# Output and query weights shared by two token tiles: a straight program in which a pair's expert rows last two steps

## The chip, the cores and the metric

The kernel runs on one core of a Trainium2 chip. The metric is the device time of one execution in microseconds (us), lower is better. The engines are TensorE (PE), VectorE (DVE), ScalarE (ACT), GpSimd (POOL) and SyncE (SP); SP, ACT and POOL issue transfers, which 16 DMA engines carry out.

## The reference

Two layers over 512 tokens of width 1024, everything in float32. Each layer is a token mixer (gated delta rule, short convolution, differential attention) with one input and one output projection, and then an expert retrieval:

```
for l in range(DEPTH):                       # 2
    proj = rms_norm(h, attn_norm[l]) @ w_in[l]              # 1024 -> 3592
    mixed = concat(gdn_mixer(...), short_conv_mixer(...), diff_attention(...))   # all causal
    h = h + mixed @ w_out[l]                                # 1024 -> 1024
    n = rms_norm(h, ffn_norm[l])
    q = n @ w_q                                             # 1024 -> 2048, 8 heads x 2 halves
    scores = q . sub_keys                                   # 2 x 128 keys for each head
    # top 16 of each half, top 16 of their 256 sums -> 128 experts per token, softmax gates
    hid = gelu(n . u_tab[idx])                              # 128 dot products per token
    h = h + sum(gate * hid * v_tab[idx])                    # 128 weighted rows per token
```

Each token has its own 128 experts, so for a tile of 128 tokens 128 gathers fetch rows of `peer_u` and 128 gathers rows of `peer_v`, each of 128 x 1024 floats (0.524 MB). Eight tiles (two layers of four) make 2048 such gathers, 1074 MB.

## The kernel before

**Tiles and steps.** Step t (0 to 7) computes the mixer and the expert choice of tile t; tiles 0 to 3 are layer 0, tiles 4 to 7 layer 1. The gathers of tile t are consumed beside step t+1 and, after step 7, in a tail of their own. Steps 0 and 1 are written out, steps 2 to 7 are a loop with two steps in its body, "lead" (2, 4, 6) and "follow" (3, 5, 7), and step 8 is the tail.

**Rows.** POOL gathers into a ring of 16 slots (`ring`), in a fixed order, each time a slot is free. A U row (from `peer_u`) is consumed by one dot product on DVE (`dot`, L1109). V rows (from `peer_v`) are consumed four at a time, as a unit, by eight matmuls on PE (`rows_v`, L810); their coefficients need all 64 dots of a half tile, a gelu, gates, and blocks that ACT writes (L507).

**What sets the order.** A string in `PLAN` says for each kind of step at which named place of the mixer U rows, V units and the small steps stand: L, H (row numbers of a half tile for the V gathers, ACT), G (gelu), C (coefficients), S (add the sums). `mix(name)` on each engine issues what the plan has there. POOL takes the rows in just that order. Engines run their own instructions strictly in order, and meet at the end of each step (`meet`).

**One step**, in the stretches that the text names:
- *projection*: norm, then `w_in` in 8 blocks of 449 columns. A lead step does it for two tiles, t and t+1, with one load of the weights; a follow step has none. Step 0 does its own tile, and tile 1 at its end.
- *conv*: convolution taps and gates, up to the transposes of the convolved values.
- *delta*: the delta rule's triangular inverse, six levels of small matmuls (L796) with DVE and ACT between.
- *attention*: state update, then four heads; logits over all 512 key positions, with a window of the bias strip copied by ACT (L606).
- *output*: `w_out`, 2 blocks; residual; second norm.
- *query*: `peer_wq`, 4 blocks, then transposes and key scores.
- *select*: top 16 searches and index arithmetic on DVE (`select`, L1117 to L1372), in two halves.

**Weights.** SP streams all weights through a ring of four slots (`wring`, L364), two transfers for each block: 16 for `w_in`, 4 for `w_out`, 8 for `peer_wq`. In before each tile's output and query blocks are loaded for that tile alone; ACT loads the keys once per step.

Of the kernel before, what the change touches and what calls it, by code (L numbers as in the profile page):

```python
# [38 lines left out]
STRIP = 896  # L39
# [7 lines left out]
EARLY = 4  # L47
# [3 lines left out]
W_ITEMS = 28  # L51

PG, PA, P_CW, P_SW, P_ON, P_QG, P_SUB, P_NA, P_DT, P_LAM, P_OFF = 0, 1024, 1032, 1080, 1086, 1214, 1278, 1342, 1346, 1350, 1351
P_W = 1352
# [4 lines left out]
PROJ = {"solo": (["nT0", "nT1"] + [f"pj{b}" for b in range(4)], [f"pj{b}" for b in range(4, 8)]),  # L59
        "lead": (["nT0", "nT1", "kT0", "kT1"] + [f"{n}{b}" for b in range(4) for n in ("pj", "pk")], [f"{n}{b}" for b in range(4, 8) for n in ("pj", "pk")]),  # L60
        "follow": ([], [])}
MIXERS = (["sT0", "sT1", "gcum", "grow"]
          + ["cN0", "cN1", "cN2", "qhT", "khT", "kbT", "kk", "qk", "qgT", "X0"]
          + [f"{n}{m}" for m in range(1, LEVELS - 1) for n in ("X", "D", "DT")] + ["dT", "X6", "DT6"]
          + ["wT", "vn", "oo", "sn", "lg00", "lg01", "yT", "lg10", "lg11"]
          + [n for h in range(2) for n in (f"aT{h}", f"lg{h+2}0", f"lg{h+2}1", f"pv{h}")] + ["aT2", "pv2", "aT3", "pv3", "zT"]
          + ["op0", "op1", "mT0", "mT1"] + [f"wq{i}" for i in range(4)] + [f"qT{i}" for i in range(4)] + [f"sc{i}" for i in range(4)])

SELECT = "sc:G r0:V r1:V r2:CV r3:V r5:V r9:V r11:V r13:V r15:V r17:V r20:V r21:V"
PLAN = {
    "first": "n0:LVVVVVVVVVVVVUUUUUU pj0:UUUU pj1:UUUU pj2:UUUU pj3:UUUU xT:UUU pj4:UUU pj5:UUU pj6:UUU pj7:UUU conv:UUU cN:UUU kbT:UUU X0:UUU "
            "L1:UUUU L2:UUUU L3:UUUU L4:UUUU L5:UUUG L6:SUU wT:C vn:UUV sn:UV y:V at1:UUUUUV at2:UUUUUV at3:UUUUUV pv3:UUUUUV op0:UUUUUUUUH op1:UUUUUV nm:UU "
            "wq0:UUUUU wq1:UUUUU wq2:UUUUU wq3:UUUUU " + SELECT,
    "lead": "n0:L n1:UUUUUUUU pj0:UUUUUUU pj1:UUUUUUUV pj2:UUUUUUU pj3:UUUUUUUV xT:U pj4:UUUU pj5:UUUUV pj6:UUUUV pj7:UUUUUUUUU conv:V "
            "cN:UV kbT:UV X0:V L1:UUUV L2:UV L3:UV L4:UGV L5:U L6:UUS wT:C vn:UUUUUV sn:V y:V at1:UUUUUV at2:UUUUUV at3:UUUUU pv3:UUUUU op0:UUUUUUUUH op1:UUUUUV nm:U "  # L80
            "wq0:UUUUUU wq1:UUUUUV wq2:UUUUU wq3:UUUUV " + SELECT,
    "follow": "n0:LUUUUUUV pj0:UUUU pj1:UUUU pj2:UUUU pj3:UUUU xT:UUV pj4:UU pj5:UUV pj6:UU pj7:UUV conv:UUV cN:UUV kbT:UUV "
              "X0:UUV L1:UUUV L2:UU L3:UUV L4:UU L5:UUV L6:UUU vn:UUUUUUU sn:UUUV y:GSC at1:UUUUVV at2:UUUUUVV at3:UUUUUVV pv3:UUUUU op0:UUUUUUUUUHV op1:UUUUUU nm:UU "
              "wq0:UUUUUUU wq1:UUUUUUU wq2:UUUUUUU wq3:UUUUUUUV " + SELECT,
    None: "end:L" + "UUUUUV" * 12 + "UUUUGUUUUSHUUUUC" + "UUUUV" * 14 + "GVVC" + "V" * NV}


def sequence(plan, first=False):

    out, row, n = [], 0, dict.fromkeys("ULHGCS", 0)  # L90
    n["V"] = EARLY
    for part in plan.split():
        where, kinds = part.split(":")
        for kind in kinds:
            if not (first and kind == "V" and n["V"] < NV):
                out.append((where, kind, n[kind], row))
# [6 lines left out]
def rows_of(seq):
    return [(kind, n) for _, kind, n, _ in seq for _ in range({"U": 1, "V": UNIT}.get(kind, 0))]


ORDER = {**{m: sequence(PLAN[m]) for m in PLAN}, "first": sequence(PLAN["first"], True), "solo": []}
LAST = rows_of(ORDER["first"])[-SLOTS:]
assert all(rows_of(ORDER[m])[-SLOTS:] == LAST for m in ("lead", "follow"))

# [15 lines left out]


def build(nc, x, rel_bias, attn_norm, w_in, gdn_conv, gdn_a_log, gdn_dt_bias, gdn_out_norm, sc_conv, diff_q_norm,
# [7 lines left out]
    with ctx:  # L136
# [3 lines left out]
        def sem(name):  # L140
# [9 lines left out]
        n2A = sb("n2A", D)  # L150
# [11 lines left out]
        carry = sb("carry", PAIRS)  # L162
# [4 lines left out]
        idxU, idxR = sb("idxU", K, i32), sb("idxR", K, i32)  # L167
        gateU, hid, coefR = (sb(n, K) for n in ("gateU", "hid", "coefR"))
# [1355 lines left out]
```

## Time and profile before

| | |
|---|---|
| median of 3 runs | 3429.05 us (3428.15 to 3433.24) |
| profiled execution, span | 3422.5 us |
| busy: PE / DVE / POOL / ACT | 2081.0 / 2265.7 / 2008.6 / 858.5 us |
| DMA | 1275.65 MB, mean 373 GB/s; the gathers 1075.38 MB of it |
| steps 0, 1 | 293.5, 357.3 us |
| steps 2, 3, 4 | 411.5, 376.0, 419.0 us |
| steps 5, 6, 7 | 376.7, 421.8, 371.8 us |
| tail | 394.9 us |

A step ends where DVE copies the normed tile for the dot products (L1424). The rows further down are windows of the trace between such points: for each the busy time of the engines with their instruction counts, the clock that was granted to TensorE (1.00 is 2.4 GHz, 0.50 is 1.2 GHz), the busy share of the DMA engines (full is 1.03 by this count) and the rate.

### The profile page before, as it was taken

What the parts mean: (1) busy time and instruction counts of PE and PEld (TensorE: products, weight loads), DVE (VectorE), ACT (ScalarE), POOL (GpSimd) and SP (SyncE); (2) the same over time, 40 slices, a digit from 0 to 9 for tenths busy, and PEclk for the clock granted to TensorE, in tenths of its full rate; (3) what the DMA queues carried; (4) which work ended last, traced back from release to release, by engine and by line L of the source; (5) the groups of instructions that cost most, each with busy time, mean ns of one, the idle gap of its engine ahead of it and who ended that gap; (6) DMA issues with size and microseconds to landing.
All of it is one profiled execution on the core that took longest, in us unless ns stands there. A gap on an engine that the chain in (4) does not pass through costs nothing.

```text
span 3422.5 us, 33690 instructions
## 1 busy us (share of the span) xinstructions
PE 2081.0 (61%) x9182; PEld 959.1 (28%) x9182; DVE 2265.7 (66%) x5019; ACT 858.5 (25%) x2516; POOL 2008.6 (59%) x2086
## 2 busy tenths in 40 slices
PE   7684466596673655497674556578776365633235
PEld 4541432244320322143331232133432132200001
DVE  3439965866759775775759876766677786675540
ACT  3311241322322230322313231223322232210111
POOL 1005454656647765665657766565665776577675
PEclk9797678698786878799787677889878687865666
DMA  9169789999999999999999999999999999999999
GB/s 300 71 208 391 238 318 401 385 400 406 378 402 409 405 353 402 405 366 404 378 402 408 407 350 405 405 363 401 369 394 405 409 391 373 406 409 409 411 409 362
DMA packets 395336, 1275.65 MB, mean 373 GB/s; under 512 B 37523, under 2 KB 78553, under 8 KB 393857
## 3 DMA queue, kind: packets, MB, share of 16 engines
q0 software_dynamic: 295744, 1075.38, 80.1%
q1 hardware_dynamic: 97808, 187.52, 15.1%
q10 hardware_dynamic: 1584, 10.47, 0.8%
q8 instruction: 80, 1.31, 0.2%
q14 instruction: 120, 0.98, 0.1%
HBM read 1266.24 MB, written 6.98 MB: 372 GB/s over the span
## 4 chain that ended last, share of the span: by engine, by line
DMA 29%; PE 24%; DVE 20%; issue 12%; POOL 11%; ACT 4%; PEldq 0%; POOLq 0%; DVEq 0%; ACTq 0%; SPq 0%; PEld 0%
DMA ring<-in_peer_v,idxR 13%; PE work L823 12%; POOL ring L438 11%; DVE ring L1109 8%; DMA ring<-in_peer_u,idxU 7%; DMA wring<-in_peer_wq 5%; PE accs L810 4%; DMA wring<-in_w_in 4%; PE work L796 3%; PE work L787 2%; DVE proj L1121 1%; PE work L934 1%; DVE proj L1117 1%; ACT arena L479 1%; DVE arena L1287 1%
## 5 line engine op out<-in xcount | busy, mean ns | idle before, releaser
L1109 DVE CUSTOM_DVE_ANT_0 ring<-ring,n2U 128x1024 f32<-128x1024 f32 x1024 | 1214.3, 1219 | 425.0 <-DMA ring<-in_peer_u,idxU 396.2
L438 POOL DMA_INDIRECT ring<-in_peer_u,idxU x1024 | 989.3, 966 | 758.1 <-issue 286.5
L438 POOL DMA_INDIRECT ring<-in_peer_v,idxR x1024 | 1002.9, 979 | 611.5 <-issue 267.9
L810 PE MATMUL accs<-ring,wv 128*32 128x512 f32 x4096 | 719.7, 838 | 737.3 <-DMA ring<-in_peer_v,idxR 698.0
L823 PE MATMUL work<-wring,nT 128*128 128x512 f32 (+1 forms) x1408 | 669.8, 633 | 122.8 <-DMA wring<-in_peer_wq 86.4
L810 PEld LDWEIGHTS accs<-ring,wv 128*32 128x32 f32 x4096 | 148.7, 135 | 1226.0 <-issue 1083.5
L823 PEld LDWEIGHTS work<-wring,nT 128*128 128x128 f32 x1408 | 289.3, 211 | 492.8 <-issue 377.8
L507 ACT ACTIVATE wv<-stack,coefR 128x32 f32<-128x32 f32 x1024 | 237.8, 309 | 379.1 <-PE accs L810 374.1
L479 ACT ACTIVATE arena<-work 128x512 f32<-128x512 f32 (+1 forms) x208 | 116.7, 588 | 462.8 <-PE work L787 236.2
L479 ACT ACTIVATE proj<-work 128x512 f32<-128x512 f32 (+1 forms) x120 | 68.1, 581 | 534.9 <-PE work L823 517.8
L1117 DVE MAX8 proj<-proj 128x8 f32<-128x128 f32 x256 | 52.7, 278 | 162.0 <-ACT proj L479 161.2
L787 PE MATMUL work<-ident,arena 128*128 128x128 f32 x296 | 61.1, 356 | 146.5 <-DVE arena L1296 107.0
L823 PE MATMUL work<-wring,arena 128*128 128x449 f32 x384 | 148.8, 540 | 0.0
L796 PE MATMUL work<-arena 128*128 128x128 f32 x768 | 109.6, 297 | 33.0 <-issue 22.8
L787 PE MATMUL work<-ident,proj 128*128 128x128 f32 x360 | 58.8, 314 | 113.2 <-DVE proj L1145 51.5
L796 PEld LDWEIGHTS work<-arena 128*128 128x128 f32 x768 | 99.0, 206 | 53.8 <-issue 42.0
L823 PEld LDWEIGHTS work<-wring,arena 128*128 128x128 f32 x384 | 72.8, 190 | 72.2 <-issue 72.2
L787 PEld LDWEIGHTS work<-ident,arena 128*128 128x128 f32 x296 | 45.8, 186 | 167.9 <-DVE arena L1296 121.7
L787 PEld LDWEIGHTS work<-ident,proj 128*128 128x128 f32 x360 | 47.0, 161 | 141.5 <-DVE proj L1145 55.7
L1109 DVE DVE_READ_ACCUMULATOR2_ANT hid<- 128x1 f32 x1024 | 84.4, 82 | 0.0
L1287 DVE CUSTOM_DVE_ANT_0 arena<-work,arena 128x512 f32<-128x512 f32 x64 | 44.3, 692 | 57.8 <-PE work L934 53.9
L681 ACT ACTIVATE idxR<-idxU 32x16 int32<-32x16 int32 x256 | 58.2, 227 | 83.4 <-DVEq L1393 49.3
(264 smaller groups left out, 2083.7 us busy)
## 6 DMA issues: line engine op xcount, KB each, us to landing
wring<-in_w_in SPq DMA_DIRECT2D x80, 898.0 KB, 15.7
wring<-in_peer_wq SPq DMA_DIRECT2D x64, 1024.0 KB, 20.0
wring<-in_w_out SPq DMA_DIRECT2D x32, 1024.0 KB, 19.9
ring<-in_peer_u,idxU POOLq DMA_INDIRECT x1024, 11.5
ring<-in_peer_v,idxR POOLq DMA_INDIRECT x1024, 12.0
arena<-keys_scr ACTq DMA_DIRECT2D x8, 1024.0 KB, 8.9
strip_scr<-ring SPq DMA_DIRECT2D x4, 512.0 KB, 8.2
keys_scr<-ring SPq DMA_DIRECT2D x2, 1024.0 KB, 5.0
```

The costliest lines, as they stand in the source:

```text
L438: nc.gpsimd.indirect_dma_start(ring[:, s * D:(s + 1) * D], None, table, bass.IndirectOffsetOnAxis(ap=idx, axis=0)).then_inc(row_in[s], 16)
L479: nc.scalar.activation(dst, s, ACT.Copy, **kw).then_inc(free[BANK[mode[0]][name][0]], 1)
L507: nc.scalar.activation(wv[:, d * QUARTER:(d + 1) * QUARTER], stack[:], ACT.Copy, scale=coefR[:, kk:kk + 1]).then_inc(blocks_ready, 1)
L681: ins = nc.scalar.activation(halves(dst, c)[quarter(o), q, :], src[quarter(q), columns(c, o)], ACT.Copy)
L787: ins = nc.tensor.transpose(w[:, i * P:(i + 1) * P], s, ident[:])
L796: ins = nc.tensor.matmul(w[:, i * P:(i + 1) * P], l, r, start=True, stop=True)
L810: ins = nc.tensor.matmul(acc[c][quarter(r), :], wv[:, d * QUARTER:(d + 1) * QUARTER], ring[:, s * D + 512 * c:s * D + 512 * c + 512], star ...
L823: ins = nc.tensor.matmul(w[:, 0:n], left[:, kc * P:(kc + 1) * P], wslot(i, n)[:, k, :], start=(kc == 0), stop=(kc == 7))
L934: filled(name, nc.tensor.matmul(w[:], qTa[o:o + 32, b * P:(b + 1) * P], keyT[o:o + 32, b * SEQ:(b + 1) * SEQ], start=True, stop=True))
L1109: V.tensor_tensor_reduce(out=rw, in0=rw, in1=n2U[:], scale=1.0, scalar=0.0, op0=ALU.mult, op1=ALU.add, accum_out=hid[:, kk:kk + 1]).then_i ...
L1117: ins = V.max(out=vals[:, 16 * i + o:16 * i + o + 8], in_=src[:, w * i:w * i + w])
L1287: link(V.tensor_tensor_reduce(out=lgs[:, o:o + 512], in0=w[:], in1=win[:, 512 * h:512 * h + 512], scale=1.0, scalar=-3e38, op0=ALU.add, op ...
```

## The change

1. The loop is gone: all eight steps and the tail are written out, with tables by tile (`order_of_banks`, `WEIGHTS`) in place of registers.
2. Output weights, query weights, key load, scores and selection of tiles 2+3, 4+5 and 6+7 are done together at the end of steps 3, 5 and 7 (`TAILS`, `stage_t`). Steps 2, 4 and 6 end after attention. Tiles 0 and 1 keep a pass of their own. In step 3, 5 or 7 one weight block serves two products, one for each tile.
3. Since the experts of both tiles are known only at the end of the pair, the gathers of a pair last over the next two steps. Rows consumed by step, tail last: before 0, 208, 256, 256, 256, 256, 256, 256, 304; now 0, 208, 121, 183, 192, 320, 192, 320, 512.
4. Attention takes only the keys up to the tile's own end: 128, 256, 384 or 512 wide for the four tiles of a layer. The window copies of ACT are gone, as DVE reads the strip directly.
5. Second buffers for what two tiles hold at once (`n2B`, `yscB`, `idxU1`, `gateU1`).

```diff
+FRONT = {0: (0,), 2: (2, 3), 4: (4, 5), 6: (6, 7)}
+BACK = {0: (1,)}
+TAILS = {0: (0,), 1: (1,), 2: (), 3: (2, 3), 4: (), 5: (4, 5), 6: (), 7: (6, 7)}
...
+LEAD = ("n0:RR n1:U8 pj0:U7 pj1:U7 pj2:U7 pj3:U7 xT:U pj4:U5 pj5:U5 pj6:U5 pj7:U5 conv:U3 cN:U2 kbT:U2G X0:U2 L1:U3C L2:U3V L3:U3V L4:U3V L5:U3V L6:U3V "
+        "vn:U6V sn:U3V y:UV at1:U6V2 at2:U6V2 at3:U6V2 pv3:U6V2 turn:U10G ")
+FOLLOW = ("n0:NCRVVU4 pj0:U4V pj1:U4V pj2:U4V pj3:U4V xT:U2V pj4:U4V pj5:U4V pj6:U4V pj7:U4V conv:U3V cN:U3V kbT:U3V X0:U3V L1:U3V L2:U3 L3:U3S L4:U3R L5:U2G L6:U2 "
+          "vn:U5C sn:U2V y:UV at1:U5V2 at2:U5V2 at3:U5V2 pv3:U4V op0:U8 op1:U8 nm:U wq0:U6 wq1:U6 wq2:U6 wq3:G sc:CNV "
+          "r0:V r1:V r2:V r3:V r5:V r7:V r9:V r11:V r13:V r15:V r17:V r20:V r21:V s0:V s1:V s3:V s5:V s7:V s9:V s11:V s13:V s15:V turn:S ")
...
+    2: "n0:R n1:U6 pj0:U3V pj1:U3V pj2:U3V pj3:U3V xT:U pj4:U3V pj5:U3V pj6:U3V pj7:U3V conv:U2V cN:UV kbT:U2V X0:UV L1:U3 L2:U3 L3:U2 L4:U2 L5:U2 L6:US "
+       "vn:U4R sn:U2 y:U at1:U4 at2:U4G at3:U4C pv3:U4",
+    3: "n0:U3 pj0:U pj1:UV pj2:U pj3:U xT: pj4:UV pj5:U pj6:U pj7:U conv:UV cN:U kbT:UV X0:U L1:U L2:UV L3:U L4:UV L5:U L6:U vn:U2V sn:U y:U at1:U at2:U2V at3:U2 pv3:U "
+       "op0:U6 op1:U6 nm:U wq0:U4 wq1:U3 wq2:U3 wq3:G sc:CN r0:V r1:V r2:V r3:V r5:V r9:V r11:V r13:V r15:V r17:V r20:V r21:V "
+       "s0:V s1:V s3:V s5:V s7:V s9:V s11:V s13:V s15:V s17:V s20:V turn:S",
+    4: LEAD, 5: FOLLOW, 6: LEAD, 7: FOLLOW,
+    8: "end:RR" + "U64" + "GU4C" + "U4V" * 15 + "NGVRU4C" + "U4V" * 15 + "GVSRU4C" + "U4V" * 15 + "GVC" + "V16S",
...
-            with sp.Fori(2, PAIRS - 1, 2) as j:
-                weights(j, "lead")
-                weights(j + 1, "follow")
...
+            def product(kind, b, who, left, n):
...
+                i0 = FIRST_ITEM[kind, b, who[0]]
+                for k in who:
+                    w = fill(f"{kind}{b}.{k}")
...
+                        if k == who[-1]:
+                            ins.then_inc(w_used, 1)
...
+        def keys_wide(k):
+            return P * (k % TILES + 1)
```

In these strings `R` is a half tile's row numbers (before: L and H), `N` the copy of the normed tile for the dots, a digit repeats the letter ahead of it, `r0` to `r21` are the places of the first tile's selection and `s0` to `s21` those of the second.

**TensorE at the end of a pair's second step.** `wring` are query weights, `proj` and `projB` the queries that are transposed, `arena` their products with the keys, `accs` the V units. Before (steps 3, 5, 7; all four query blocks, then on):

```order
L820 REGISTER_ALU
L823 MATMUL work<-wring,nT 128x512 x16
L820 REGISTER_ALU
L823 MATMUL work<-wring,nT 128x512 x16
L804 ISA
L806 ISA
L810 MATMUL accs<-ring,wv 32x512 x8
L787 MATMUL work<-ident,proj 128x128 x16
L796 MATMUL work<-arena 128x128 x16
L804 ISA
L806 ISA
L810 MATMUL accs<-ring,wv 32x512 x8
```

Now, in step 3 (the last three of the four query blocks):

```order
L836 MATMUL work<-wring,nT 128x512 x8
L836 MATMUL work<-wring,arena 128x512 x8
L836 MATMUL work<-wring,nT 128x512 x8
L836 MATMUL work<-wring,arena 128x512 x8
L836 MATMUL work<-wring,nT 128x512 x8
L836 MATMUL work<-wring,arena 128x512 x8
L800 MATMUL work<-ident,proj 128x128 x16
L809 MATMUL work<-arena 128x128 x16
L800 MATMUL work<-ident,projB 128x128 x16
L809 MATMUL work<-arena 128x128 x16
L823 MATMUL accs<-ring,wv 32x512 x192
```

Each query block is now two products, the transposes and scores come twice, no V unit stands among them, and 24 units (192 matmuls) follow in one piece beside the two selections.

**TensorE at the end of the program.** Before:

```order
L804 ISA
L810 MATMUL accs<-ring,wv 32x512 x8
L1060 REGISTER_ALU
L273 REGISTER_ALU
L273 COMPARE_AND_BRANCH
L810 MATMUL accs<-ring,wv 32x512 x352
L136 UNCONDITIONAL_BRANCH
```

Now:

```order
L836 MATMUL work<-wring,arena 128x512 x8
L800 MATMUL work<-ident,proj 128x128 x16
L809 MATMUL work<-arena 128x128 x16
L800 MATMUL work<-ident,projB 128x128 x16
L809 MATMUL work<-arena 128x128 x16
L823 MATMUL accs<-ring,wv 32x512 x696
L195 UNCONDITIONAL_BRANCH
```

Of the units behind the last loop step there were 44 (352 matmuls), all in the tail; of the 87 (696) now, 23 stand beside the selections of step 7 and 64 in the tail.

## Rows read from the trace of the kernel before

**Rows 1.** A window for each step, of all engines; steps 4 and 5 left out.

```profile
core 0: us, PE busy (x) PEld busy (x) DVE busy (x) ACT busy (x) POOL busy (x), PEclk, DMA share, GB/s
0.00:293.50 293.50, 226.71 (x818) 133.22 (x818) 139.59 (x410) 78.85 (x155) 31.49 (x54) 0.90 0.65 216
293.50:650.80 357.30, 185.67 (x820) 96.22 (x820) 276.60 (x617) 89.68 (x254) 198.96 (x205) 0.71 0.91 343
650.80:1062.30 411.50, 302.99 (x1276) 142.32 (x1276) 282.06 (x627) 114.60 (x332) 247.81 (x255) 0.84 1.01 394
1062.30:1438.30 376.00, 202.50 (x1000) 90.96 (x1004) 280.92 (x618) 96.75 (x292) 250.96 (x255) 0.77 1.00 394
...
2234.00:2655.80 421.80, 303.06 (x1272) 142.97 (x1268) 282.93 (x626) 114.80 (x332) 249.48 (x257) 0.83 0.99 386
2655.80:3027.60 371.80, 203.84 (x1020) 90.62 (x1015) 280.67 (x618) 96.39 (x292) 255.72 (x261) 0.78 1.00 396
3027.60:3422.50 394.90, 147.03 (x704) 28.67 (x704) 159.22 (x261) 55.99 (x235) 273.47 (x292) 0.63 1.00 399
```

**Rows 2.** A window in the tail: the rate of gathers alone.

```profile
3045.00:3345.00 300.00, 99.14 (x456) 18.99 (x452) 146.32 (x239) 39.07 (x163) 216.90 (x232) 0.62 1.03 410
```

**Rows 3.** DMA issues by line: count, size of one, us to landing.

```profile
wring<-in_w_in SPq DMA_DIRECT2D x80, 898.0 KB, 15.7
wring<-in_peer_wq SPq DMA_DIRECT2D x64, 1024.0 KB, 20.0
wring<-in_w_out SPq DMA_DIRECT2D x32, 1024.0 KB, 19.9
...
arena<-keys_scr ACTq DMA_DIRECT2D x8, 1024.0 KB, 8.9
```

**Rows 4.** Windows of step 0, without rows: delta, attention, scores.

```profile
80.00:129.00 49.00, 32.45 (x202) 29.11 (x200) 27.84 (x42) 12.19 (x25) 0.00 (x0) 0.79 0.35 125
129.00:172.80 43.80, 26.29 (x140) 19.18 (x140) 19.30 (x52) 20.24 (x43) 0.00 (x0) 0.74 0.12 48
...
226.50:232.00 5.50, 3.92 (x34) 3.67 (x33) 0.00 (x0) 3.26 (x6) 0.00 (x0) 1.00 0.70 243
```

**Rows 5.** Windows of step 1: conv stretch and before, delta, attention.

```profile
293.50:354.60 61.10, 8.63 (x38) 6.17 (x39) 55.08 (x89) 15.75 (x33) 35.80 (x34) 0.58 0.96 362
354.60:435.10 80.50, 38.79 (x202) 35.01 (x200) 73.41 (x127) 16.73 (x42) 36.19 (x38) 0.67 0.72 245
435.10:502.20 67.10, 43.55 (x220) 19.75 (x220) 43.56 (x94) 25.24 (x72) 38.17 (x41) 0.71 0.82 306
```

**Rows 6.** Windows of step 6: projection, delta, attention, select; then step 3's delta.

```profile
2257.00:2369.00 112.00, 109.70 (x332) 52.08 (x333) 78.19 (x125) 20.88 (x43) 67.38 (x70) 0.97 1.02 394
...
2380.00:2444.00 64.00, 42.08 (x312) 27.22 (x309) 46.82 (x73) 21.09 (x63) 42.87 (x44) 0.92 1.03 408
2444.00:2509.00 65.00, 42.77 (x188) 20.97 (x188) 43.76 (x96) 23.60 (x65) 38.60 (x40) 0.61 0.91 343
...
2596.00:2655.80 59.80, 28.82 (x180) 6.50 (x176) 57.82 (x227) 18.54 (x70) 39.71 (x41) 0.79 1.03 407
...
1133.80:1197.30 63.50, 42.59 (x298) 27.99 (x296) 52.83 (x85) 16.48 (x45) 48.86 (x49) 0.89 1.02 403
```

**Rows 7.** Timeline of TensorE: projection of two tiles starts; output; query; V unit.

```profile
665.94 9.29 PE L823 MATMUL work<-wring,nT 128*128 128x449 f32 x16 [1.72 <-ACT arena L488]
...
174.05 15.47 PE L823 MATMUL work<-wring,nT 128*128 128x512 f32 x32 [0.52 <-issue]
...
197.02 29.66 PE L823 MATMUL work<-wring,nT 128*128 128x512 f32 x64 [0.73 <-issue]
...
2265.89 6.20 PE L823 MATMUL work<-wring,arena 128*128 128x449 f32 x16
...
2284.11 1.92 PE L810 MATMUL accs<-ring,wv 128*32 128x512 f32 x16
```

**Rows 8.** Groups by line and shape: the dot product.

```profile
L1109 DVE CUSTOM_DVE_ANT_0 ring<-ring,n2U 128x1024 f32<-128x1024 f32 x1024 | 1214.3, 1219 | 425.0 <-DMA ring<-in_peer_u,idxU 396.2 <-ACTq L703 5.5 <-PEq L1059 4.4
```

More of the change, by code:

```diff
@@ L50 @@
 WSLOTS = 4
[L51 to L67, printed above, removed]
@@ L88, in sequence @@
[L88 to L96, printed above, removed]
+PG, PA, P_CW, P_SW, P_ON, P_QG, P_SUB, P_NA, P_DT, P_LAM = 0, 1024, 1032, 1080, 1086, 1214, 1278, 1342, 1346, 1350
+P_W = 1351
+MODE = ("solo", "follow") + ("lead", "follow") * 3
@@ L97, in sequence, with schedule @@
+def schedule():
+    out, row = {}, 0
+    per_tile = {"U": K, "V": 2 * NV, "R": 2, "G": 2, "C": 2, "S": 1, "N": 1}
+    n = dict.fromkeys(per_tile, 0)
+    for t in range(PAIRS + 1):
+        out[t] = []
+        for part in PLAN[t].split():
+            where, kinds = part.split(":")
+            for kind in each(kinds):
+                out[t].append((where, kind, n[kind] // per_tile[kind], n[kind] % per_tile[kind], row))
+                n[kind] += 1
                 row += {"U": 1, "V": UNIT}.get(kind, 0)
-            n[kind] += 1
@@ L99, in sequence @@
-    assert n["U"] == K and n["V"] in (2 * NV + EARLY, 3 * NV) and [n[k] for k in "LHGCS"] == [1, 1, 2, 2, 1] and row % SLOTS == 0
-    return out
[L103 to L109, printed above, removed]
+    assert all(n[k] == PAIRS * per_tile[k] for k in n), n
@@ L209, in build @@
+        full = [sem(f"bank_full{b}") for b in range(BANKS)]
+        free = [sem(f"bank_free{b}") for b in range(BANKS)]
         row_in = [sem(f"row{r}") for r in range(SLOTS)]
@@ L438, in gather, with step @@
                 nc.gpsimd.indirect_dma_start(ring[:, s * D:(s + 1) * D], None, table, bass.IndirectOffsetOnAxis(ap=idx, axis=0)).then_inc(row_in[s], 16)
-            def step(t, a, gathered, first=False):
-                if not gathered:
-                    return
-                before, seen = rows_of(order(a, first)), {}
-                for _, kind, n, row in order(a, first):
+            def step(t):
+                for _, kind, k, n, row in ORDER[t]:
                     if kind == "U":
@@ L885, in stage_a @@
+                flip(f"qgT.{k}", blocks(qn, 4))
+                pe.wait_ge(S["mx_ready"], nth("mx_ready", k))
+                heads(f"X0.{k}", [(mxa[:, h * P:(h + 1) * P], ident[:]) for h in range(GH)])
                 mix("X0")
@@ L1043, in _, with step @@
             pe.sem_inc(met, 1)
-            def step(t, a, gathered, first=False):
-                mode[0] = a
-                turn(a, first)
+            def step(t):
                 def mix(name):
-                    if not gathered:
+                    if t == 0:
                         prepare(name)
-                    for where, kind, n, row in order(a, first):
-                        if gathered and where == name and kind == "V":
-                            rows_v(t, first, n, row)
-                if not a:
+                    for where, kind, k, n, row in ORDER[t]:
+                        if where == name and kind == "V":
+                            rows_v(k, n, row)
+                if t == PAIRS:
                     mix("end")
```

1054 lines of the change are left out of this document (539 added, 515 removed), and 2 rows, old and new, of the table PLAN.

## The prediction

> **What bounds the kernel now.** I read the windows by step first. From step 2 to the end the DMA engines are busy 0.99 to 1.01 of the time at 386 to 399 GB/s, and in the tail, where nothing but gathers runs, 1.03 at 410 GB/s [rows 1, 2]. DVE is busy for about 280 of some 375 to 420 us in these steps, PE for 200 to 300 [rows 1]. So the transfers set the time of steps 2 to 8, and only steps 0 and 1 (216 and 343 GB/s) are set by their chains of work. A gathered row costs 0.5243 MB / 0.410 = 1.28 us of full rate [rows 2].
>
> Then I looked for the length of a step where it has little to gather, since the change makes such steps. Step 0 has no rows at all: delta 49.0 us, attention 43.8 us, with DVE busy 27.8 and 19.3 us of these [rows 4]. Here PE, ACT and DVE wait for each other in turn. Each row consumed inside adds to this chain: in step 1 delta takes 80.5 us with 30 dots, (80.5 - 49.0) / 30 = 1.05 each; in step 6 64.0 with 11 dots and 7 V units, 0.83 each; in step 3 63.5 with 20 and 6, 0.56 each [rows 5, 6]. Attention: step 1 67.1 with 23 and 7, 0.78 each; step 6 65.0 with 25 and 5, 0.71 each [rows 5, 6]. One dot is 1.22 us [rows 8], so little of it hides.
>
> **What the change removes.** Three passes of 4 + 8 weight transfers of 1024 KB (1.049 MB) and three of eight key loads of that size [rows 3]: 39 x 1.049 = 40.9 MB, 102 us at 0.40 MB/us, the rate of stretches with weights in them [rows 1]. The bill from step 2 on at full rate, after: 1840 rows x 1.28 = 2355, 48 loads of `w_in` (0.920 MB) x 2.3 = 110, 36 x 2.62 = 94, three key loads 8, in all 2567 us; before it was 2669, and took 3422.5 - 650.8 = 2771.7 [rows 1], so about 100 us, the end included, went unused.
>
> The Trainium skill (Perfetto Trace Analysis, section Identifying the Most-Contended Engine) says to relieve the engine with the highest use first; by that rule the 102 us would be the gain. The rows agree on which resource it is; whether it stays so in each step is counted below. The same page of the Trainium skill, section Optimization Strategy, advises to interleave stretches with different limits, and this change separates them.
>
> **What it moves.** The plan's counts: steps 2 and 3 consume 121 + 183 = 304 rows for 512 before, steps 4+5 and 6+7 still 512, the tail 512 for 304. 208 rows go from beside the mixers of steps 2 and 3 to the tail, where nothing hides them. What do steps 2 and 3 take without them?
>
> *Step 2.* Norms until the first projection product: 665.9 - 650.8 = 15 us [rows 1, 7]. Projection 112 [rows 6]: PE is busy for 110 of it, its blocks 2 x 6.2 us [rows 6, 7]; 7 V units for 4 add 3 x 1.9 [rows 7] = 6. Conv stretch 11 us in step 6 (between its windows of 2257 to 2369 and 2380 on, rows 6), take 12. Delta with 17 dots and 3 units: 49 + 20 x 0.65 = 62 (0.56 to 1.05 each: 60 to 70). Attention with 23 dots, 384 keys wide: 44 + 23 x 0.8 = 62, less 3 for the width, plus 4 for the row numbers and coefficients that ACT writes there = 63. End 4. Sum **274 us**. Its transfers would need 121 x 1.28 + 16 x 2.3 = 192, so DMA idles for some 80 us.
>
> *Step 3.* Up to the end of the conv stretch step 1 takes 61.1 with 40 dots [rows 5]; now 12 dots and 3 units: 28 dots fewer at 0.8 to 1.22 give 27 to 39, take 36 with the units. Delta, 9 + 3: 49 + 8 = 57. Attention, 11 + 2, full width: 44 + 10 = 54. Output: 15.5 us for one tile [rows 7], 31 for two; the second norm ends 5 us after the products for one tile, two share ACT, take 10: 41. Query: 29.7 for one tile [rows 7], 59 for two, and 4 for transposes. Scores of the first tile 5.5 [rows 4]; those of the second lie beside the selection. Selection: 59.8 us with DVE busy 57.8 of it [rows 6], twice: 120. End 3. Sum **380 us** against transfers of 183 x 1.28 + 12 x 2.62 + 3 = 268. The selections hold 96 rows, 123 us, and stay full; the output and query stretches, 110 us, hold 23 rows and 12 loads, 61 us.
>
> Steps 2+3 together: 654, before 411.5 + 376.0 = 787.5 [rows 1], **-133**. Of their transfer time of 460, nearly 200 us of DMA are left idle, twice what the removed loads save.
>
> *Steps 4+5, 6+7.* Lead step: 19 (as step 2, and 4 more for row numbers) + 104 (112 without its 4 units) + conv 15 + delta with 29 consumptions, dense on DVE, 49 + 29 x 0.93 = 76 + attention with 45, 44 + 34 = 78, less 10 (128 keys) or 4 (384) + 10 dots at the end 15: 297 and 303. In step 6 of before the loop's jump back shows as a start of 23 us for 15 (2234 to 2257, rows 1 and 6); that is gone here. Follow step: up to attention 193 rows, 247 us of transfers against a chain of some 225, take 243; then output 41, query 63, scores with copies and a V unit 11, selection 120, end 3: 481. Pairs: 778 and 784, before 795.7 (two steps alike left out of the rows) and 421.8 + 371.8 = 793.6 [rows 1]. **-27** together, not the 68 of removed loads, since in the 110 us of output and query there are 35 rows and 12 loads (76 us) and a ring that is at most 20 us ahead.
>
> *Tail.* 394.9 + 208 x 1.28 = **661, +266** [rows 1, 2]. PE (147 of 395 us busy) and DVE (159) stay far from a limit, with the same eight-row pattern.
>
> *Steps 0 and 1.* Attention is 128 and 256 wide for 512, and ACT's copies go. In the 43.8 us of step 0 [rows 4] I take 9 off (4 to 14); in step 1 the ring is full again from there on, 4 (0 to 9). **-13.**
>
> The second copies and buffers, the per-tile tables and missing register work cost nothing where transfers or a chain bind; I take 0 (up to 5 us either way).
>
> Sum: 3422.5 - 133 - 27 + 266 - 13 = **3515.5** for the span. The median of the runs lies 6.55 above the span, so **3522 us**, 2.7% slower.
>
> **The rivals.**
> - *Bytes are time (faster).* If every step stayed full, the 102 us come off: 3429 - 102 - 13 = 3314. It speaks for it that DMA is at its limit in every step now [rows 1]; against it that step 2 would have to end in 192 us while its projection alone needs 127. This is what the rule cited above from the Trainium skill (Perfetto Trace Analysis) would give. Chance 2%.
> - *Short chains (faster).* The rows inside hide as in step 3's delta, and pairs 4+5 and 6+7 come near their transfer time. Step 2 is then 15 + 104 + 10 + 49 + 41 + 17 = 236 at the least, step 3 345, the pairs 745 each: 3422.5 - 206 - 99 + 266 - 20 + 6.5 = 3370. It turns to a gain once steps 2 to 7 together are 93 us shorter than in my sum. For it: two tiles' chains meet fewer rows than any row of the trace shows beside step 0. Against: 0.56 is the lowest of five prices. Chance 7% for under -0.2%, and 3% for a stop within 0.2%.
> - *Longer still.* PE's clock was 0.61 in the attention of step 6 and 0.74 in step 0's [rows 4, 6]; if starved stretches keep it at 1.2 GHz in the doubled products too, 87 us of output and query in each pair cost up to twice as much: half of that is 130 us, 3650. Against: the solo products of step 0 ran at full pace after just such an attention [rows 7]. Chance 8% for over 3585.
>
> **How the numbers follow.** Forecast 80%: 3455 to 3585, from delta and attention at 0.56 to 1.05 per consumption (-25 to +35 over six steps), the transfer-bound part of the follow steps (up to 20 us of ring each, -40 to +10), steps 0 and 1 (-10 to +9). What a measurement can tell from no change is about 0.2%. Faster 0.09, same 0.03, slower 0.88; the predicted time is the forecast's, and the range 3455 to 3585 leaves out some 2 in 10.
>
> **What would show it.** In the changed profile: 40.9 MB less; step 2 near 274 us with the rate near 280 GB/s, step 3 near 380 with 290; output and query of steps 3, 5, 7 with PE over 0.9 busy and DMA under full; selections of 120 us; a tail of 661 us at 410 GB/s, with 64 units. I am wrong if step 2 and 3 sum to under 600, or if the pairs take under 740, since the chains then hide more than step 1 showed.

## The result and the profile after

The changed kernel takes 3552.7 us (3549.5 to 3554.8), beside 3428.6 us of the kernel before: a ratio of 1.036, 95% interval 1.0346 to 1.0375. It is slower by 3.6%; 3522 us were predicted, with a range of 3455 to 3585. The profiled execution spans 3547.5 us.

These are the windows by step of the changed kernel, in the columns of [rows 1], and one more in its tail, which answers to [rows 2]. The line from 2884.00 on is the tail. Here steps 3, 5 and 7 end with DVE's addition of the sums (L1420), steps 4 and 6 with the dot before the copy of the second tile (L1453), step 2 with attention.

```profile
core 0: us, PE busy (x) PEld busy (x) DVE busy (x) ACT busy (x) POOL busy (x), PEclk, DMA share, GB/s
0.00:277.90 277.90, 214.92 (x777) 127.21 (x778) 133.87 (x405) 71.52 (x151) 31.20 (x52) 0.90 0.67 220
277.90:635.50 357.60, 187.64 (x803) 96.10 (x801) 273.03 (x614) 84.86 (x250) 197.48 (x203) 0.70 0.91 341
635.50:886.00 250.50, 183.71 (x790) 102.37 (x790) 151.68 (x275) 75.27 (x201) 125.82 (x127) 0.83 0.91 338
886.00:1247.90 361.90, 247.59 (x1158) 120.93 (x1158) 253.25 (x705) 92.92 (x258) 178.57 (x176) 0.81 0.80 289
1247.90:1566.80 318.90, 200.56 (x832) 106.03 (x832) 210.45 (x383) 78.97 (x227) 182.34 (x192) 0.79 0.93 358
1566.80:2064.90 498.10, 293.19 (x1388) 127.04 (x1388) 340.41 (x856) 121.28 (x389) 315.91 (x323) 0.77 0.95 370
2064.90:2384.50 319.60, 203.46 (x856) 106.36 (x856) 213.56 (x382) 81.75 (x227) 181.17 (x190) 0.80 0.92 354
2384.50:2884.00 499.50, 297.30 (x1412) 127.86 (x1412) 343.41 (x857) 123.74 (x389) 314.85 (x323) 0.76 0.93 361
2884.00:3547.50 663.50, 212.29 (x1024) 41.84 (x1024) 314.92 (x520) 91.59 (x389) 470.28 (x502) 0.59 1.01 402
...
2900.00:3500.00 600.00, 188.81 (x888) 36.91 (x892) 298.26 (x492) 78.24 (x336) 437.49 (x467) 0.57 1.03 410
```

No step from 2 to 7 keeps the DMA engines full any more: 0.80 to 0.95, where [rows 1] had 0.99 to 1.01. The tail runs at the rate of [rows 2] and is about as long as its 512 rows (512 x 1.28 = 655).

| | before | predicted | after |
|---|---|---|---|
| steps 0+1 | 650.8 | 638 | 635.5 |
| steps 2+3 | 787.5 | 654 | 612.4 |
| steps 4+5 | 795.7 | 778 | 817.0 |
| steps 6+7 | 793.6 | 784 | 819.1 |
| tail | 394.9 | 661 | 663.5 |
| span | 3422.5 | 3515.5 | 3547.5 |

The count of 183 rows in step 3 is that of the kernel; the diff of the change above shows its plan with one dot less at `at1` (the kernel has `at1:U2`) and without `r7:V`.

From the page, the transfers and the weights' way (three groups of DMA issues, answering to [rows 3]), and the two dearest waits:

```profile
DMA packets 375573, 1231.47 MB, mean 347 GB/s; under 512 B 36866, under 2 KB 77896, under 8 KB 374512
...
L1133 DVE CUSTOM_DVE_ANT_0 ring<-ring,n2U 128x1024 f32<-128x1024 f32 x1024 | 1210.8, 1219 | 451.1 <-DMA ring<-in_peer_u,idxU 419.7
...
L453 POOL DMA_INDIRECT ring<-in_peer_v,idxR x1024 | 995.3, 972 | 701.0 <-issue 281.3
...
wring<-in_w_in SPq DMA_DIRECT2D x80, 898.0 KB, 8.3
wring<-in_peer_wq SPq DMA_DIRECT2D x40, 1024.0 KB, 12.1
wring<-in_w_out SPq DMA_DIRECT2D x20, 1024.0 KB, 13.4
```

44.2 MB less are moved, 40.9 of them the shared weights and keys, at 347 for 373 GB/s.

Now the stretches, which answer to [rows 4 to 6]. Step 2: projection, delta, attention. Step 3: output, query, and both selections.

```profile
650.50:765.00 114.50, 114.49 (x380) 52.90 (x380) 46.00 (x71) 23.91 (x58) 57.20 (x58) 0.98 1.00 375
...
771.00:831.30 60.30, 37.52 (x251) 28.53 (x249) 54.15 (x89) 13.26 (x29) 37.17 (x37) 0.83 0.92 353
831.30:886.00 54.70, 21.76 (x96) 14.98 (x96) 42.03 (x96) 22.98 (x66) 21.61 (x23) 0.57 0.67 220
...
1023.30:1065.00 41.70, 35.12 (x82) 16.59 (x82) 24.55 (x43) 5.04 (x11) 13.32 (x14) 0.83 0.87 303
1065.00:1120.00 55.00, 54.31 (x127) 24.21 (x128) 10.66 (x20) 6.05 (x10) 9.11 (x10) 1.00 0.61 212
...
1131.00:1247.90 116.90, 63.80 (x389) 14.16 (x387) 110.34 (x422) 27.20 (x111) 86.86 (x89) 0.80 0.98 389
```

Projection and query are PE's alone (busy 114.49 of 114.50, 54.31 of 55.00), the selections DVE's (110 of 117), and DMA idles beside attention and query. That is the chain-bound pair that was forecast. Steps 4 and 5 are different: delta and attention of step 4, then of step 5 all up to conv's end, delta, attention, output and query.

```profile
1377.20:1460.50 83.30, 43.91 (x282) 32.68 (x280) 64.13 (x109) 24.61 (x72) 40.11 (x42) 0.75 0.73 264
1460.50:1555.80 95.30, 46.39 (x249) 16.70 (x249) 52.78 (x118) 17.82 (x67) 71.80 (x78) 0.70 1.03 409
1566.80:1690.60 123.80, 45.64 (x222) 12.62 (x223) 69.27 (x112) 31.87 (x107) 89.85 (x91) 0.64 1.01 396
1690.60:1766.30 75.70, 45.48 (x266) 34.78 (x265) 59.73 (x96) 18.08 (x50) 48.32 (x48) 0.76 0.90 346
1766.30:1844.10 77.80, 39.65 (x229) 15.16 (x229) 48.08 (x107) 25.74 (x92) 52.98 (x57) 0.73 0.94 358
1844.10:1885.50 41.40, 34.13 (x87) 16.29 (x84) 27.89 (x49) 5.29 (x11) 23.84 (x25) 0.89 1.03 406
1885.50:1940.30 54.80, 54.80 (x128) 24.20 (x129) 19.30 (x34) 5.72 (x9) 16.11 (x18) 1.00 0.92 351
```

Within one step the limit changes from stretch to stretch. In step 4's delta POOL starts only 42 gathers in 83 us and DMA is at 0.73: the ring's slots are taken, and POOL waits 44.1 us for dots to free them. In its attention no engine is busy over 0.76 of the time, POOL included, but DMA is full, and DVE waits 29.5 us for rows. The two waits (total us, times, longest):

```profile
POOL ring L453 <- DVE hid L1133: 44.1, 9, 16.3
...
DVE ring L1133 <- DMA ring<-in_peer_u,idxU: 29.5, 4, 8.7
```

### The profile page after: what moved, and what is told of

It reads as the page before. It is cut to its first block, busy times and chain, and to the rows that moved or that the text cites. A ratio compares the mean times of both kernels' runs of the same rounds, so it can differ in the third digit from the quotient of the medians.

```text
span 3547.5 us, 30818 instructions
## 1 busy us (share of the span) xinstructions
PE 2040.7 (58%) x9038; PEld 955.7 (27%) x9038; DVE 2234.6 (63%) x4995; ACT 821.9 (23%) x2481; POOL 1997.6 (56%) x2084
## 4 chain that ended last, share of the span: by engine, by line
PE 31%; DVE 25%; POOL 15%; DMA 13%; issue 12%; ACT 4%; POOLq 0%; DVEq 0%; ACTq 0%
PE work L836 19%; POOL ring L453 15%; DVE ring L1133 8%; DMA ring<-in_peer_v,idxR 7%; PE accs L823 4%; PE work L809 4%; DMA ring<-in_peer_u,idxU 3%; DMA wring<-in_w_in 3%; PE work L800 2%; DVE projB L1145 1%; DVE projB L1141 1%; ACT arena L488 1%; DVE proj L1145 1%; DVE arena L1257 1%; ACT coefR L690 1%
## 5 line engine op out<-in xcount | busy, mean ns | idle before, releaser
L823 PE MATMUL accs<-ring,wv 128*32 128x512 f32 x4096 | 748.4, 869 | 940.0 <-DMA ring<-in_peer_v,idxR 873.0
L836 PE MATMUL work<-wring,nT 128*128 128x449 f32 (+1 forms) x1024 | 448.0, 593 | 33.9 <-DMA wring<-in_w_in 18.5
L836 PE MATMUL work<-wring,arena 128*128 128x512 f32 (+1 forms) x736 | 313.7, 577 | 11.7 <-DMA wring<-in_peer_wq 10.4
L836 PEld LDWEIGHTS work<-wring,nT 128*128 128x128 f32 x1024 | 203.1, 202 | 266.6 <-issue 240.2
L488 ACT ACTIVATE arena<-work 128x512 f32<-128x512 f32 (+3 forms) x224 | 120.2, 563 | 473.4 <-PE work L800 258.2
L836 PEld LDWEIGHTS work<-wring,arena 128*128 128x128 f32 x736 | 142.3, 194 | 174.4 <-issue 164.4
L488 ACT ACTIVATE proj<-work 128x512 f32<-128x512 f32 (+1 forms) x88 | 49.0, 576 | 279.3 <-PE work L836 275.4
L488 ACT ACTIVATE projB<-work 128x449 f32<-128x449 f32 (+1 forms) x64 | 36.6, 572 | 316.3 <-PE work L836 312.4
L809 PE MATMUL work<-arena,proj 128*128 128x128 f32 x384 | 68.1, 332 | 62.8 <-ACT arena L488 62.8
L1133 DVE DVE_READ_ACCUMULATOR2_ANT hid<- 128x1 f32 x1024 | 84.3, 82 | 0.0
L809 PEld LDWEIGHTS work<-arena,proj 128*128 128x128 f32 x384 | 58.3, 233 | 81.9 <-ACT arena L488 71.1
```

Source lines behind the costliest of these rows:

```text
L488: nc.scalar.activation(dst, s, ACT.Copy, **kw).then_inc(free[BANK[name][0]], 1)
L809: ins = nc.tensor.matmul(w[:, i * P:(i + 1) * P], l, r, start=True, stop=True)
L823: ins = nc.tensor.matmul(acc[c][quarter(r), :], wv[:, d * QUARTER:(d + 1) * QUARTER], ring[:, s * D + 512 * c:s * D + 512 * c + 512], star ...
L836: ins = nc.tensor.matmul(w[:, 0:n], left(k, kc), wslot(i, n)[:, kc % 4, :], start=(kc == 0), stop=(kc == 7))
L1133: V.tensor_tensor_reduce(out=rw, in0=rw, in1=n2U[:], scale=1.0, scalar=0.0, op0=ALU.mult, op1=ALU.add, accum_out=hid[:, kk:kk + 1]).then_i ...
```

## The experiments

Where nothing else is said, the kernel before took 3425.9 to 3429.2 us beside them.

**The single-tile kernel in a straight program.** `TAILS` gives each tile its own output, query and selection again, and the plan is that of the kernel before (L and H written R).

```diff
-TAILS = {0: (0,), 1: (1,), 2: (), 3: (2, 3), 4: (), 5: (4, 5), 6: (), 7: (6, 7)}
+TAILS = {t: (t,) for t in range(8)}
...
+    2: LEAD1, 3: FOLLOW1, 4: LEAD1, 5: FOLLOW1, 6: LEAD1, 7: FOLLOW1,
...
```

> The straight program and the narrow attention alone: each tile has its own output, query and selection pass again, and the order of rows is that of the kernel before (256 rows in each of steps 2 to 7, 304 in the tail). Theory A (the pairs cost all of the loss): before less 13 to 16 us for the narrow attention of steps 0 and 1 and less 2 x 7 us for the loop's jumps back, 3400 us (3385 to 3415). Rival C (the straight program or the new buffers cost something themselves): above 3430 us, up to 3550.

Measured: 3388.5 us, ratio 0.989 (0.9874 to 0.9907): 1.1% faster than the kernel before and 4.6% faster than the changed one, so all that makes the change slow is in the pairing and in the order of rows that goes with it. Its windows for steps 4 to 7 and the tail:

```profile
1420.50:1828.00 407.50, 293.96 (x1232) 139.14 (x1236) 277.05 (x623) 108.83 (x328) 244.95 (x254) 0.84 1.02 397
1828.00:2207.50 379.50, 208.48 (x1008) 94.38 (x1000) 276.69 (x615) 91.58 (x288) 255.92 (x264) 0.75 1.01 397
2207.50:2613.60 406.10, 297.37 (x1244) 139.96 (x1248) 280.62 (x623) 111.38 (x328) 242.99 (x250) 0.83 1.02 395
2613.60:2989.50 375.90, 212.41 (x1032) 94.92 (x1023) 280.54 (x616) 94.18 (x288) 259.04 (x264) 0.75 1.00 394
2989.50:3383.70 394.20, 142.99 (x704) 28.34 (x704) 159.34 (x260) 56.13 (x235) 273.50 (x292) 0.61 1.00 400
```

DMA is full in each, with all weights loaded per tile. Against this kernel the changed one stands at +164 us by the spans: steps 2+3 612.4 for 783.9, a tail of 663.5 for 394.2, together **+98**; pairs 4+5 and 6+7 817.0 and 819.1 for 787.0 and 782.0, together **+67**; steps 0 and 1 -1.

**One pair only.** The same, but tiles 6 and 7 are paired, with the plan of steps 2 and 3 and the long tail.

```diff
-TAILS = {t: (t,) for t in range(8)}
+TAILS = {**{t: (t,) for t in range(6)}, 6: (), 7: (6, 7)}
...
```

> As e3_single, but tiles 6+7 share one pass, with the plan that the changed kernel has for its first pair (steps 2 and 3) in steps 6 and 7, and its tail of 512 rows. Theory A (one shortage of rows, paid once, at the first pair wherever it stands): steps 6+7 near 612 us in place of some 775, the tail 663 for 395: about +100 us on e3_single, near 3500 us. Rival D (each pair costs the same): a third of the loss of the changed kernel against e3_single, +50 us, near 3450 us.

Measured: 3488.0 us, ratio 1.017 (1.0155 to 1.0189), 99.6 over the single kernel. Steps 6 and 7 take 250.8 and 360.6 us, 171 less than there, the tail 665.3, 271 more. Rival D (+50) is out: the 98 us come once, with the first pair wherever it stands, whose two steps have 304 rows to consume and leave 208 more to the tail.

**Width or loop?** The single kernel with attention over all 512 positions; the bias is then read at a wrong offset and future keys aren't masked.

```diff
         def keys_wide(k):
-            return P * (k % TILES + 1)
+            return SEQ
```

> The kernel of e5_wide once more (e3_single, 3388.5 us, with attention over all 512 key positions in every tile; bias read at the wrong offset in six tiles and future keys not masked, same work), since its first run fell where before took 3726 us. Theory A (a step set by transfers doesn't feel a shorter chain, only steps 0 and 1 do): step 0 gets 7 to 12 us longer, step 1 by 0 to 6, the others by under 2 each: 3403 us, between 3395 and 3412; the rest of the 39.7 us between e3_single and before is then the loop (its start in steps 4 and 6, and register work). Rival (the narrow attention made the whole gain): 3420 to 3430.

Measured: 3411.1 us, ratio 0.9957 (0.9941 to 0.9973), 22.6 over the single kernel, at the upper edge of what theory A gave; the rival is out. Step 0 is 12.0 longer, step 1 6.4, the pairs of steps 2+3, 4+5 and 6+7 by 6.5, -0.9 and -0.7: in the last two pairs a lead step's longer attention is given back in the follow step. About 23 of the 40 us are thus the narrow attention, 18 of these in steps 0 and 1. The other 15 are what else tells this kernel from the one before: the straight program and the missing window copies of ACT, which no run parts.

**The shared loads alone.** The changed kernel, but in steps 3, 5 and 7 each output and query block is loaded for each tile: 36 loads of 1.049 MB more, all else in place.

```diff
...
-                    product("op", i, tails, mixed, 512)
+                    for k in tails:
+                        product("op", i, (k,), mixed, 512)
...
-                    product("wq", i, tails, normed, 512)
+                    for k in tails:
+                        product("wq", i, (k,), normed, 512)
```

> The changed kernel, but in steps 3, 5 and 7 each output and query block is loaded twice, once for each tile of the pair (36 weight transfers of 1.049 MB more, 94 us of DMA time at 2.62 us each), with the same order of products and rows. Theory A (the saved transfers fall where the DMA engines are idle anyway): by the busy shares of the output, query and score stretches of the changed kernel, step 3 has 35 us idle there and steps 5 and 7 about 13 us each, so 0 + 18 + 18 = +37 us, 3590 us. Rival B (bytes are time): +94 us, 3647 us.

Measured: 3625.8 us, ratio 1.058 (1.0561 to 1.0596), 73.1 over the changed kernel, twice what theory A gave. Step 3 is 9.7 longer, step 5 29.6, step 7 30.9. Output and query of step 5 in this kernel:

```profile
1856.70:1906.50 49.80, 34.04 (x69) 13.68 (x66) 22.09 (x39) 1.64 (x4) 21.23 (x23) 0.88 1.03 403
1911.40:1982.10 70.70, 59.42 (x129) 25.17 (x128) 20.78 (x36) 6.77 (x11) 16.85 (x18) 0.92 1.01 370
```

Only step 3 has the idle transfer time that I counted on (0.61 in its query, as shown above). In step 5 of the changed kernel output and query stand at 1.03 and 0.92, since the ring refills there (25 gathers start in output, where 17 rows are consumed), and 12 loads cost their full 31 us in steps 5 and 7. Sharing output and query weights is worth 73 us where it stands (the keys stay shared in this run); the arrangement that it needs costs 164 + 73 = 237.

**Rows out of attention.** The changed kernel with another `LEAD`: seven dots more stand beside the projection of steps 4 and 6, four V units more beside delta, and from attention to the end there are 67 rows for 88 (the strings are cut at their start; counted in them, the 12 dots and 71 rows of the expectation are 7 and 67).

```diff
...
-pj0:U7 pj1:U7 pj2:U7 pj3:U7 xT:U pj4:U5 pj5:U5 pj6:U5 pj7:U5 conv:U3
+pj0:U8 pj1:U8 pj2:U8 pj3:U8 xT:U4 pj4:U5 pj5:U5 pj6:U5 pj7:U5G conv:U3C
...
-vn:U6V sn:U3V y:UV at1:U6V2 at2:U6V2 at3:U6V2 pv3:U6V2 turn:U10G
+vn:U5 sn:U2V y:UV at1:U6V2 at2:U6V at3:U6V pv3:U6V turn:U7G
```

> The changed kernel with another plan string for steps 4 and 6 alone: the same 192 rows, but 12 more dots beside the projection, the V units from the start of the delta rule on, and 71 rows for 88 from the attention to the end. Theory A (the ring carries only 16 rows, so idle DMA in the delta stretch, 264 GB/s, isn't given back in the attention stretch, 409 GB/s): steps 4 and 6 near 305 us for 319, together -15 to -35 us, 3528 us. Rival E (the attention stretch of 95 us is set by DVE and PE, not by transfers): within 5 us of the changed kernel.

Measured: 3509.7 us, ratio 1.024 (1.0220 to 1.0254), 43 less than the changed kernel, more than theory A gave and far from rival E. Delta and attention of step 4:

```profile
1385.50:1469.80 84.30, 53.51 (x346) 30.89 (x345) 62.04 (x105) 25.79 (x86) 52.90 (x56) 0.80 0.93 356
1469.80:1544.70 74.90, 35.47 (x184) 13.66 (x184) 52.40 (x116) 14.51 (x52) 56.78 (x60) 0.67 1.03 409
```

Delta is as long as before (84.3 us for 83.3) with DMA at 0.93 for 0.73, and attention is 20 us shorter, with 60 gathers for 78. Its plan has 39 consumptions there for 45; at the 0.78 us of [rows 5] six of them are 5 us, so the other 15 are the supply of rows, which set this stretch.

**Rows into the query stretch.** On top of that, 11 U rows of each of steps 5 and 7 go later: 4 from the front and 7 from attention, to delta (2), output (2) and query (7, where the expectation says 9). The strings are cut at their start.

```diff
...
-vn:U5C sn:U2V y:UV at1:U5V2 at2:U5V2 at3:U5V2 pv3:U4V op0:U8 op1:U8 nm:U wq0:U6 wq1:U6 wq2:U6
+vn:U3 sn:UC y:UV at1:U4V2 at2:U4V3 at3:U4V2 pv3:U3V op0:U9 op1:U9 nm:U wq0:U9 wq1:U8 wq2:U8
```

> The kernel of e9_follow_plan once more (e6_lead_plan, 3509.7 us, with 11 U rows of each of steps 5 and 7 moved: 4 out of the front and 7 out of attention, 2 to the output and 9 to the query stretch), since its first run fell where before took 3726 us. Theory A (output and query already hold full transfers, 1.03 and 0.92 of DMA, as the ring refills there, so some 4 us are free): 0 to 12 us less than e6_lead_plan, 3498 to 3510. Rival (the prediction's count, 76 us of transfers in 110, room for the 11 rows): 2 x 11 x 1.28 = 28 us less, 3482.

Measured: 3500.9 us, ratio 1.021 (1.0188 to 1.0226), 8.8 less than the kernel it starts from, as theory A gave and far from the rival's 28. Of the difference of the profiled executions (12.0) 6.6 lie in the two pairs. The front of step 5, attention and query:

```profile
1546.10:1663.60 117.50, 46.08 (x222) 13.58 (x223) 64.37 (x104) 31.91 (x107) 86.03 (x89) 0.62 1.01 399
1741.50:1819.40 77.90, 46.09 (x228) 20.29 (x228) 38.36 (x91) 25.75 (x93) 44.72 (x49) 0.68 0.78 297
1857.60:1915.10 57.50, 56.39 (x127) 24.57 (x127) 29.91 (x50) 6.51 (x11) 23.41 (x25) 0.95 1.03 402
```

The front falls from 124.2 to 117.5 us with 4 rows fewer, attention stays at 78 with seven dots fewer and DMA now at 0.78, and the query gives 2.5 back, full at once. What sets that attention now is open: transfers have room in it, yet DVE still waits 24.1 us there for rows, and POOL 20.4 us for dots that free slots. No run has a ring of more slots. The pairs are at 794 and 795 us, still 20 together above the single kernel's. The rest is an estimate. With every stretch full a pair would need 512 rows x 1.28 + 16 x 2.3 + 12 x 2.62 + 3 = 726, and to make up for the 98 us the two later pairs would have to take 735 each. That leaves under 10 us of idle transfer time for each pair; the best of the two plans leaves 68.

**Fewer bytes per row.** If transfers bind, a smaller V row must help. The changed kernel, with 1 KB for 4 KB in each gather of a V row; three quarters of each V row are left out.

```diff
+                n = D if row < SLOTS or table is uT else D // 4
+                if n < D:
+                    table = table.rearrange("e (four d) -> (e four) d", four=4)
-                nc.gpsimd.indirect_dma_start(ring[:, s * D:(s + 1) * D], None, table, ...
+                nc.gpsimd.indirect_dma_start(ring[:, s * D:s * D + n], None, table, ...
```

> The kernel of e7_short_v once more. In its own run the kernel before took 3726 us for 3428, and DVE paused 41 times, 87 us together, inside the runs of search instructions that wait for nobody, as it does in no trace of the earlier runs; so that run can't be set beside the changed kernel's 3552.7. Theory A, if before is at 3428 again: steps 2 and 3 within 5 us of 250.5 and 361.9; attention of steps 4 and 6 from 95 to some 70; the front of steps 5 and 7 from 124 to 85 to 105; steps 4+5 and 6+7 at 745 to 770; tail some 500: in all 3262 us, 3220 to 3300. Rival (the work of the consumptions, not transfers, made steps 4 to 7 longer than forecast): both pairs within 15 us of 817 and 819; 3390 us or so. If before is at 3726 again and the pauses are there, this is a property of the chip it runs on and says nothing of the two.

Measured: 3490.2 us, ratio 1.018 (1.0166 to 1.0200). 403 MB less are moved and only 62 us are gained. Steps 2 and 3 stay at 249.7 and 359.3, as theory A said; but steps 4+5 and 6+7 stay at 802.4 and 809.1, as the rival said, and the tail at 636.0, which neither gave. Both had left out a third limit. Windows of step 4's attention, of step 5's front and of the tail, then POOL's own timeline within that attention (start, duration, and in brackets the idle time ahead and what ended it):

```profile
1444.50:1538.30 93.80, 42.26 (x248) 15.93 (x248) 52.90 (x117) 17.81 (x67) 71.02 (x75) 0.73 0.72 240
1552.50:1672.50 120.00, 47.59 (x222) 13.42 (x223) 69.72 (x112) 31.74 (x107) 90.55 (x92) 0.60 0.74 244
...
2900.00:3300.00 400.00, 132.68 (x592) 25.24 (x592) 217.65 (x357) 57.24 (x247) 302.17 (x322) 0.58 0.81 280
```

```profile
1459.72 0.96 POOL L456 DMA_INDIRECT ring<-in_peer_v,idxR  x1 [0.30 <-issue]
1460.99 0.95 POOL L456 DMA_INDIRECT ring<-in_peer_v,idxR  x1 [0.30 <-issue]
1462.24 0.95 POOL L456 DMA_INDIRECT ring<-in_peer_v,idxR  x1 [0.30 <-issue]
1463.49 0.94 POOL L456 DMA_INDIRECT ring<-in_peer_v,idxR  x1 [0.30 <-issue]
1464.74 0.94 POOL L456 DMA_INDIRECT ring<-in_peer_u,idxU  x1 [0.30 <-issue]
```

POOL starts a gather every 1.25 us, 0.95 shown as busy and 0.30 as issue, whether it is of 1 KB or of 4 KB. 75 x 1.25 = 93.8, the whole stretch, with DMA at 0.72; 92 x 1.25 = 115 of the 120 us of the front, at 0.74; 512 x 1.242 = 636, the tail, at 0.81. So the rows are supplied at no more than one per 1.24 us by POOL and one per 1.28 by transfers, and the two lie so close that either alone looks like the limit. Transfers do bind beside it: the loads of the two-loads run cost their full time in steps 5 and 7. The Trainium skill (Perfetto Trace Analysis, section What "DMA-bound" means) names the issuing engine's sequencer as one of the things that can bind, to be known by solid slices; here the slices cover 0.95 of each 1.25 us and the engine binds all the same.

**Runs that decide nothing.** In five runs (the wide kernel, the paired one with short V rows and the follow plan at their first run, and the single kernel with short V rows at both of its runs) the kernel before took 3726 or 3775 us beside them, and their traces show idle time of DVE that is put down to no engine of this core (`remote`) and that the traces of the other runs don't have, also within runs of search instructions.

> The kernel of e8_short_v_single once more (e3_single, 3388.5 us, with 1 KB gathers for V rows; three quarters of each V row are left out), since its first run fell where before took 3726 us. From e11_short_v a new number: POOL starts a gather every 1.24 us at the best, whatever its size (0.94 busy and 0.30 between), next to 1.28 of transfer for a full row. So a tail of 304 rows can't end before 304 x 1.24 = 378 us. Theory A (steps 2 to 7 of the single kernel are set by bytes, 256 rows and the weights, and both POOL, 256 x 1.24 = 318 us, and the chain lie well below): lead steps 407 to 375 to 395, follow steps 377 to 340 to 360, tail 378: 3215 us, 3160 to 3270. Against 3490 of the paired kernel with short V rows it would then be ahead by 275 us, for 164 at full rows. Rival (the chains are nearly as long as the transfers, so sharing weights could not have gained its 102 us even without a shortage of rows): steps 2 to 7 lose less than 12 us each, 3300 to 3370.

| | this (us) | before beside it (us) | ratio |
|---|---|---|---|
| single, wide | 3681.0 | 3726.1 | 0.985 |
| paired, short V | 3918.2 | 3726.1 | 1.050 |
| single, short V | 3615.4 | 3726.1 | 0.969 |
| single, short V, again | 3668.4 | 3774.7 | 0.971 |
| paired, follow plan | 3910.4 | 3726.1 | 1.047 |

DVE's timeline in the last of them, within the selection of step 0:

```profile
265.31 0.42 DVE L1145 FIND_INDEX8 proj<-proj,arena 128x8 uint32<-128x256 f32 x1
268.30 0.09 DVE L1151 MATCH_VALUE_LOAD arena<-proj,arena 128x8 f32 x1 [2.56 <-remote]
268.38 0.41 DVE L1151 MATCH_REPLACE8 arena<-proj,arena 128x256 f32<-128x256 f32 x1
```

It stays open how far the single kernel's steps lie above their chains: both runs that ask it are of this kind.

## Why the prediction was right, and where it was wrong

The sign, the mechanism that gives it and the tail held; the middle of the sum did not, in two errors that took off part of each other (-42 in steps 2 and 3, +74 in the two later pairs). That the total came within 31 us is in part luck: with the second error alone it would have been near 3595, outside the range.

- *Tail*: +266 predicted, +268.6 measured, 208 more rows at 1.28. Right, although its limit is a double one: POOL alone would give 636.
- *Steps 2+3*: -133 predicted, -175 measured. The mechanism is right (they stay within 3 us when V rows shrink), the size was not. Step 2 is 250.5 for 274: start and projection 129.5 for 133, conv 6 for 12, delta 60.3 for 62, attention 54.7 for 63, end 0 for 4. Step 3 is 361.9 for 380, with 29.6 for 36 up to conv, 97 for 104 in output and query, and 117 for 123 at the end. The largest term is attention: by my own sum a consumption in it cost (54.7 - 44 + 3 - 4) / 23 = 0.42 us, below the lowest of the five prices that I had (0.56), where I took 0.8; in delta it was (60.3 - 49.0) / 20 = 0.57 for 0.65. The rest are small things (conv, end) that I added at each place. Of my nearly 200 us of idle transfer time some 150 were there (612 less 460), and step 2 ran at 338 GB/s, not 280. The rival of short chains was thus half right here (581 at the least, 612 measured, 654 predicted).
- *Steps 4 to 7*: -27 predicted, **+47** measured. This is the step that failed. I took the follow step up to the end of attention as one piece, 193 rows x 1.28 = 247 against a chain of some 225, and took the larger less a credit for the ring (243). But the ring holds 16 rows, so the larger has to be taken in each stretch. My own prices would then have given about 271: front 89 rows x 1.28 = 114, delta 49 + 29 x 0.93 = 76, attention 63 rows x 1.28 = 81. Measured were front 123.8 (DMA 1.01), delta 75.7 (0.90) and attention 77.8 (0.94), in all 277.3. The front was full from its first microsecond and DVE waited 30.5 us for rows in it, so the ring had come nearly empty from the lead step and there was no credit. The rest of step 5 was 17 us shorter than forecast (220.8 for 238). In the lead step I priced attention by its chain, 68, and it was set by its rows, 95.3; moving rows out brought it to 74.9. Delta there was 83.3 for 76, (83.3 - 49.0) / 29 = 1.18 a consumption, above the highest of the five prices. Beside the 0.42 of step 2 that shows that one price for a consumption does not carry from stretch to stretch. Where I saw room, in output and query (76 us of transfers in 110), the ring refilled: 1.03 and 0.92 in step 5.
- *Steps 0 and 1*: -13 predicted, -15.3 measured. The sum is right by luck: step 0 gave 15.6 for 9 (4 to 14), step 1 became 0.3 longer, where 4 shorter were forecast. The wide run puts 18 us on the width in these two.
- *Bytes are time*: the 40.9 MB are gone and the time is longer, and 403 MB more change the pairs by 10 to 15 us each. The Trainium skill's rule (Perfetto Trace Analysis, section Identifying the Most-Contended Engine), to relieve the busiest engine first, gave 3314. The traces agree that removing loads has a worth, 73 us for 36 of the 39 in the two-loads run, but what makes them removable costs 237.
- *Longer still*: the granted clock was 0.57 in step 2's attention and 1.00 in step 3's query, which took 55.0 us for the 59 forecast; the output before it, at 0.83, took 41.7 for 41. That rival is out. (Output and query of two tiles are 2 x (15.5 + 29.7) = 90 us by [rows 7], where I wrote 87.)
- *POOL*: the prediction doesn't name it as a limit at all; its busy share of the span before is 59%. It was 3% from one (1.24 us for 1.28).

## What to carry to other kernels

When a change saves bytes on the busiest resource but moves its work in time, draw the balance stretch by stretch, with the buffer between as the only credit: in each the longest of chain, issue of the gathers and transfers counts, and what a full buffer can't take is lost. Work that is hidden only while something runs beside it has to be repaid in full (here 208 rows, 269 us) when it slides past the end. The parts of this change that help need no slide: the straight program without the window copies and the narrow attention alone give 3388.5 us, 1.1% under the kernel before.

## What the runs showed of the hardware

- A gather of 128 rows costs POOL 1.24 to 1.25 us from start to start, 0.94 busy and 0.30 shown as issue, the same for 1 KB and 4 KB rows. Busy time alone understates it by a quarter.
- Twice the kernel before took 9 and 10% longer (3726 and 3775 us), and in the traces beside it DVE pauses by up to 7 us inside runs of search instructions that wait for no other engine of the core. Ratios between kernels aren't preserved there: the same follow plan stands at 1.047 in such a run and at 1.021 outside. The cause wasn't found.
